# Inverse roots of the norms as exp(-0.5 ln) on ScalarE, with table sets loaded ahead

## What is computed

```python
def rms_norm(x, g):
    xf = x.astype(jnp.float32)
    y = xf * lax.rsqrt(jnp.mean(xf * xf, axis=-1, keepdims=True) + EPS)
    return (y * g.astype(jnp.float32)).astype(x.dtype)

def layer_norm(x, g, b):
    xf = x.astype(jnp.float32)
    mu = xf.mean(-1, keepdims=True)
    var = jnp.square(xf - mu).mean(-1, keepdims=True)
    return ((xf - mu) * lax.rsqrt(var + LN_EPS) * g.astype(jnp.float32) + b.astype(jnp.float32)).astype(x.dtype)
```

## Time and profile before

| | us |
|---|---|
| median of three runs (lowest, highest) | 3767.95 (3752.62, 3784.52) |
| the profiled execution | 3787.55 |
| its span, from the first to the last instruction | 3785.8 |

### The profile page before, as it was taken

The page is one execution under the profiler, slowest core; times in us unless marked ns, Lnnn a source line. Parts: engine busy times, 40 slices in busy tenths (PEclk is TensorE's granted clock), DMA queues, the critical chain, the costliest instruction groups (busy, mean ns, idle before and its releaser), DMA issues. The chain is left out here.

```text
span 3785.8 us, 34815 instructions
## 1 busy us (share of the span) xinstructions
PE 3204.5 (85%) x12250; PEld 2180.1 (58%) x12250; DVE 2147.4 (57%) x3756; ACT 878.0 (23%) x2154; POOL 704.3 (19%) x679
## 2 busy tenths in 40 slices
PE   7999888797777777777777789778999899989998
PEld 6887688583232222232222377366887687668876
DVE  2323577657785764774444562345874454558753
ACT  2112332122222222222222310252220102312201
POOL 0001244003344443443333210000000000100000
PEclk6999888899999999999999999579999997699999
DMA  6657897668999999999999822001332231013321
GB/s 205 205 202 248 280 288 240 211 206 349 421 420 421 419 412 421 418 413 422 421 417 421 342 73 84 0 1 67 95 98 86 70 120 34 1 62 97 97 88 68
DMA packets 154291, 845.76 MB, mean 223 GB/s; under 512 B 15328, under 2 KB 15584, under 8 KB 87584
## 3 DMA queue, kind: packets, MB, share of 16 engines
q0 software_dynamic: 83392, 578.06, 37.5%
q1 hardware_dynamic: 70752, 265.79, 22.0%
HBM read 841.70 MB, written 136.31 MB: 258 GB/s over the span
## 5 line engine op out<-in xcount | busy, mean ns | idle before, releaser
L752 PE MATMUL PS<-AR,HC 128*128 128x512 f32 x1536 | 726.8, 618 | 251.0 <-ACT HC L1190 250.6
L198 PE MATMUL PS<-AR_r,RHI 128*128 128x512 f32 x1888 | 761.4, 403 | 96.0 <-DVE AR_r L1359 60.0
L200 PE MATMUL PS<-AR_r,RING_r 128*128 128x512 f32 x1888 | 745.9, 395 | 0.0
L752 PEld LDWEIGHTS PS<-AR,HC 128*128 128x128 f32 x1536 | 283.3, 194 | 693.6 <-ACT HC L1190 398.6
L1544 DVE SCALAR_TENSOR_TENSOR AR<-AR 128x1024 f32<-128x1024 f32 x384 | 469.9, 1224 | 359.4 <-DMA AR<-peer_uv,XC 358.6
L199 PE MATMUL PS<-AR_r,RHI 128*128 128x512 f32 x1504 | 594.1, 395 | 0.0
L457 POOL DMA_INDIRECT AR<-peer_uv,XC x384 | 402.3, 1048 | 737.4 <-PE PS L752 543.3
L198 PEld LDWEIGHTS PS<-AR_r,RHI 128*128 128x128 f32 x1888 | 362.2, 192 | 183.8 <-issue 87.4
L1341 DVE CAST RHI<-RING 128x1024 fp32r<-128x1024 f32 x256 | 178.7, 698 | 466.9 <-DMA RING<-in_wstream 463.6
L200 PEld LDWEIGHTS PS<-AR_r,RING_r 128*128 128x128 f32 x1888 | 361.7, 192 | 77.2
L199 PEld LDWEIGHTS PS<-AR_r,RHI 128*128 128x128 f32 x1504 | 287.9, 191 | 64.6 <-issue 6.0
(11 more groups left out here) (333 smaller groups left out, 3779.9 us busy)
## 6 DMA issues: line engine op xcount, KB each, us to landing
RING<-in_wstream SPq DMA_DIRECT2D x304, 512.0 KB, 3.6
peer_uv<-in_peer_u SPq DMA_DIRECT2D x48, 1024.0 KB, 12.7
peer_uv<-in_peer_v SPq DMA_DIRECT2D x48, 1024.0 KB, 13.0
peer_uv<-in_peer_v POOLq DMA_DIRECT2D x16, 1024.0 KB, 22.2
peer_uv<-in_peer_u POOLq DMA_DIRECT2D x16, 1024.0 KB, 22.3
AR<-peer_uv,XC POOLq DMA_INDIRECT x384, 13.5
XL<-in_xl SPq DMA_DIRECT2D x1, 2048.0 KB, 9.9
RHI_f<-peer_uv,XC POOLq DMA_INDIRECT x128, 13.5
```

What stands on the lines that cost most here:

```text
L198: pe.matmul(out, sh, mh, start=start, stop=False)
L200: return pe.matmul(out, sl, mh, start=False, stop=stop)
L752: mm = pe.matmul(bank(2 * (tt % 2) + x), DIAG[:, n % NDIAG, :], ROWS_UV[n % NROW][:, D + 512 * x:D + 512 * x + 512], start=(j == 0), stop= ...
```

## The change

`root` becomes an Ln with the same scale and bias, a wait of ScalarE for itself, and an Exp with scale -0.5 in place. What it writes is the inverse root, so all wide reciprocals of VectorE go: in `finish`, in n1 and the context's norm, for both sets of four heads, and for the difference attention's 24 and 8 columns. `preload_act_table_set` puts a table load at a chosen place: the set that has both Ln and Exp is loaded at the start of each `rms` and `layer_norm`, after the Silu of n1, and ahead of both norms of heads; the set that has Silu is loaded ahead of the feed-forward loops. The stick-breaking and the difference attention follow on places where the first of these is held. In the difference attention the root of the first six heads moves from step 30 to step 29 of ScalarE's loop, and the semaphore `root` counts 1 and 2 in place of 1 to 3.

```diff
--- before.py
+++ after.py
@@ -46,6 +46,7 @@
 EPS, LN_EPS = 1e-6, 1e-5
 MASKED = -1e30
 LN_MIN = 2.0 ** -63
+LN_EXP, SILU = "natural_log_exp_and_others", "silu_and_others"
 
 BLK = 8
 NSLOT = 4
@@ -470,7 +471,7 @@
                 barrier(pool, n)
             pool.dma_start(STRIP, t["strips"]).then_inc(s_strip, 16)
             barrier(pool, 15)
-            pool.wait_ge(df["root"], 2)
+            pool.wait_ge(df["root"], 1)
             for h in range(DHALF):
                 for ib in range(TT):
                     o = DO[:, h, P * ib:P * ib + P]
@@ -1009,9 +1010,13 @@
                 act.wait_ge(chunk_used, c + 1)
 
             def root(out, src, scale, eps):
-                return act.activation(out, src, ACT.Sqrt, scale=scale, bias=par(eps))
+
+                steps.done(act.activation(out, src, ACT.Ln, scale=scale, bias=par(eps)))
+                steps.wait()
+                return act.activation(out, out, ACT.Exp, scale=-0.5)
 
             def rms(s, gain, shift, to):
+                act.preload_act_table_set(LN_EXP)
                 for k in range(KT):
                     after(act, s, "res", k + 1, KT)
                     act.activation(ar(S * k, S), XL[:, k, :], ACT.Square).then_inc(s["sq"], 1)
@@ -1268,6 +1277,7 @@
                     act.wait_ge(u["evac"], g * BLK + (2 * FT * l + 4 + x + 1))
                     act.activation(HL[:, x, :], HL[:, x, :], ACT.Silu).then_inc(u["sg"], 1)
 
+                act.preload_act_table_set(SILU)
                 with act.Fori(0, 2 * FT // BLK) as g:
                     for j in range(4):
                         pair(g, j)
@@ -1307,7 +1317,7 @@
                         act.activation(DP[i % 2][x][:, 0:n], bank(2 * (i % 2) + x, 0, n), ACT.Exp,
                                        bias=DNM[:, 2 * i + x:2 * i + x + 1],
                                        accum_out=DRS[:, 2 * i + x:2 * i + x + 1]).then_inc(df["exp"], 1)
-                if i == TT * DHALF + 6:
+                if i == TT * DHALF + 5:
                     head_root(0, DHALF)
                 if 1 <= i <= n_df:
                     k = i - 1
@@ -1369,8 +1379,6 @@
             def finish(s, src, name, x, parts):
 
                 after(dve, s, "root", 1, 1)
-                steps.done(dve.reciprocal(STAT[:], STAT[:]))
-                steps.wait()
                 for k in range(KT + 2):
                     if k < KT:
                         dve.tensor_tensor(HL[:, k, :], src[:, k, :], STAT[:], ALU.mult).then_inc(s["scaled"], 1)
@@ -1392,12 +1400,9 @@
 
             dve.wait_ge(s_in, 80)
             dve.wait_ge(n1["root"], 1)
-            steps.done(dve.reciprocal(STAT[:], STAT[:]))
-            dve.wait_ge(ctx_root, 1)
-            steps.done(dve.reciprocal(SMALL[:], SMALL[:]))
-            steps.wait()
             for k in range(KT):
                 dve.tensor_tensor(HL[:, k, :], XL[:, k, :], STAT[:], ALU.mult).then_inc(n1["scaled"], 1)
+            dve.wait_ge(ctx_root, 1)
             for k in range(KT):
                 dve.tensor_tensor(HC[:, k, :], XC[:, k, :], SMALL[:], ALU.mult).then_inc(ctx_scaled, 1)
             dve.wait_ge(chunk_used, FIRST["mod1"] + 16)
@@ -1507,8 +1512,6 @@
             for h in range(HG_HEADS):
                 o, r = HLF[:, 512 * h:512 * h + 512], EW[:, 512 * h:512 * h + 512]
                 dve.wait_ge(ho["root"], h + 1)
-                steps.done(dve.reciprocal(r, r))
-                steps.wait()
                 steps.done(dve.tensor_tensor(o, o, r, ALU.mult))
                 steps.wait()
                 dve.scalar_tensor_tensor(MIX[:, 4 + h, :], o, par("hg_norm")[:, h:h + 1], G[:, h, :], ALU.mult, ALU.mult)
@@ -1690,8 +1693,6 @@
                                          ).then_inc(rt["dev"], 1)
             for h in range(RET_HEADS):
                 dve.wait_ge(rt["root"], h + 1)
-                steps.done(dve.reciprocal(RST[:, h, :], RST[:, h, :]))
-                steps.wait()
                 steps.done(dve.tensor_tensor(RO[:, h, :], RO[:, h, :], RST[:, h, :], ALU.mult))
                 steps.wait()
                 dve.tensor_tensor(MIX[:, h, :], RO[:, h, :], RG[:, h, :], ALU.mult)
@@ -1843,16 +1844,10 @@
                         ins = dve.scalar_tensor_tensor(DJUNK[ib], o, 1.0, o, ALU.mult, ALU.mult,
                                                        accum_out=DSS[:, TT * h + ib:TT * h + ib + 1])
                     ins.then_inc(df["squares"], 1)
-                if i == TT * DHALF + 7:
-                    dve.wait_ge(df["root"], 1)
-                    dve.reciprocal(DROOT[:, 0:TT * DHALF], DROOT[:, 0:TT * DHALF]).then_inc(df["root"], 1)
                 if n_df - ahead <= i < n_df:
                     split_chunk(FIRST["out_o"] + i - (n_df - ahead))
 
-            dve.wait_ge(df["root"], 3)
-            last = DROOT[:, TT * DHALF:TT * DIFF_HEADS]
-            steps.done(dve.reciprocal(last, last))
-            steps.wait()
+            dve.wait_ge(df["root"], 2)
             for h in range(DHALF, DIFF_HEADS):
                 for ib in range(TT):
                     o = DO[:, h, P * ib:P * ib + P]
```

## The result

The changed kernel takes 3721.2 us (median of 4 runs, 3713.24 to 3739.23), the kernel before 3776.23 (4 runs, 3752.62 to 3791.85). The ratio is 0.9842, with a 95% interval of 0.9807 to 0.9878: 1.6% less, some 60 us; the two medians are 55.0 us apart. The predicted 3723.5 is met within 2.3 us, but partly by luck: the predicted saving was 44.5 from a median of 3767.95, and one run added to the three known ahead lifts that median by 8.3. The profiled execution took 3727.29 us, its span 3725.5 against 3785.8: 60.3 less.

The account below looks back on a forecast made before the run. TensorE was busy for 85% of the span; the change pays in norms where it stands still. Terms 13.5 + 5.4 + 14.2 + 6.9 + 3.8 + 0.4 + 0.3 = 44.5 us, from 3767.95 to 3723.5, range 3698 to 3746.

Parts of the forecast that it names:

- Part 1: n2 and layer norms 0 to 2: root ready before VectorE finishes its splits, so the full reciprocal goes; 13.5 us.
- Part 2: nf and last layer norm: VectorE waits for the root, Exp takes the reciprocal's place; 2.7 each, 5.4 us.
- The price by the rows: Table loads: 1.28 us each, next instruction 0.01 later, without an added drain; so the load ahead of nf fits.
- Part 3: Norms of four heads in series lose load and reciprocals from the chain: retention 14.2 us, the scan's gated norm 6.9.
- The scan's heads: Gated norm ahead of the output projection: same chain as the retention's, but a chunk landing limits the gain to 6.9 us.
- the third of these landed 10.3 us later: Third chunk of the output weights: issued at 675.19, landed at 685.5, a time kept for the changed kernel.
- next in line is nearer: Rival, 0.17: scan's chunks later (5.5 lost), attention starts no sooner (3.8), semaphores at seven norms (1.4); about 34 us gained.
- first term: Scan's norm: chunks land later, as with the fourth chunk, losing 5.5 of the 6.9 us.
- Part 4: Stick-breaking attention: 17 loads, 21.8 us of ScalarE, go; only 3.8 on the path, 2.57 at the head, 1.27 later.
- That is 1.27 more: Stick-breaking attention: in one head of seven a load ends later than the weights; removing it gains 1.27 us.
- the rival with a rising clock: Stick-breaking attention: TensorE's clock rises with shorter pauses, 10 us more, 54 in all, 3713 us; chance 0.18.
- Part 5: Edits worth little: feed-forward loops lose 20 loads for 0.4 us, difference attention gains 0.3, other sites 0.

Follow-up runs that it names:

- stat_only: The kernel before with only the norms of the tokens changed (n2, nf, four layer norms: Ln and Exp, set loaded at each one's start): 3780.51 us.
- two_loads: The changed kernel with two table loads more in each of the six norms of the tokens, behind the wait for the sum: 3718.46 us, profiled.
- copies_only: The changed kernel with three expert table pieces moved from behind the output weights' first chunks to behind the experts' first chunks, keys unmoved: 3748.69 us.
- rt_only: The kernel before with only the retention's norm of heads changed, and the Exp-only set loaded again behind it: 3787.49 us.
- no_preload: The changed kernel with all six preloads left out, so a load comes where a function needs it: 3757.6 us, ratio 0.9925.
- loads_only: The kernel before, norms unchanged, with only the table sets loaded ahead of the stick-breaking attention and the feed-forward loops: 3781.35 us.
- control: The kernel before, unchanged, profiled once more: 3801.39 us, span 3799.6.
- two_loads_again: The changed kernel with two more loads in each of the six token norms, profiled a second time and timed: 3750.52 us, ratio 0.9895.
- keys_later: The changed kernel with GpSimd fetching the expert keys only when the first chunk of the output weights is used: 3741.39 us, ratio 0.9857.
- copies_early: The changed kernel with three expert table pieces moved from behind the output weights' first chunks to behind chunks of the second modulation: 3736.75 us, ratio 0.9839.

## Why the prediction was right, and where it was not

**Part 1, reciprocals behind the chunk splits: right.** Four norms, 3.3 to 3.4 each, and stat_only gives them alone. The slack read above, 0.45 and 2.28 us, which two_loads bears out, is what the part relied on: the Exp is done before VectorE asks.

**Part 2, behind the root: right.** 2.7 twice. The load ahead of nf fitted in: it stands at 2150.06 for 1.28 us, and the squares follow at 2151.61, released by VectorE, not by the load. The price by the rows held; that of the Trainium skill (ScalarE: Activation LUTs, What ACT_TABLE_LOAD costs), by which the load would have stuck out by about 1 us, did not.

**Part 3, the retention's heads: right** (14.3, forecast 14.2), alone and in the whole. **The scan's heads: the right chain, a wrong size.** The step that failed is "the third of these landed 10.3 us later", kept for the changed kernel. Forecast 6.9, measured 3.8: the chunk took 13.4. The prediction held fixed a transfer whose neighbours move: the keys' 1 MB follow the same barrier as VectorE's splits. copies_only shows that transfers hold that wait (7.3 without the three pieces). Of the 3.1 us the keys are some 2.6: at the same spacing of issues, with the same pieces but the keys behind, rt_only's chunk took 10.8. The other 0.5 go with the closer spacing, or are the scatter of such landings (10.3 to 11.0 in the six profiles in which the keys come behind the landing or 1.2 us ahead of it). And no_preload's step of 4.0 has another end than the changed kernel's 3.8: VectorE's chain in the one, the landing in the other. So the rival "next in line is nearer" was right in its first term, with 3.1 of the 5.5 us that it had for it; its other two, 3.8 and 1.4, did not come: TensorE did start the attention's work sooner, and the seven norms show no such loss.

**Part 4, loads in the stick-breaking attention: right at the head, right elsewhere in the number only.** 4.0 in loads_only for 3.8, although ScalarE's busy time falls by 20.5 us there: the loads were covered by TensorE. The head's 2.6 are the two loads. The step "That is 1.27 more" failed: rt_only, stat_only and no_preload keep that load and have 1.39 us of wait there like the rest, so the prediction took for a cost of the load what came from where the low clock fell in two profiles (before and control). In the whole change the attention gives 5.0 to 5.3, at a granted clock of 0.77 in place of 0.75; that is 1.2 us of TensorE's busy time (81.99 to 80.77), and the rival with a rising clock had 10.

**Part 5: right as far as it can be seen.** In the changed kernel the loops are within 0.5 us of before, but for the last down-projection, 1.4 shorter where the unchanged control is 1.5 shorter. The largest difference otherwise is 1.3 us, in two_loads_again.

**The sum.** The steps add to 42.0 for 43.8, one error of 3.1 and the stick-breaking's 1.1 the other way; without the 2.4 of the stick-breaking's rest, of which 1.5 to 2.2 come with the loads kept (rt_only, stat_only), the edits have 39.6. The remaining 18 us of the profiled pair stand at no edit. 7.3 are in the first 650 us, where the control gains 3.6 and the profiles with the changed kernel's code up to there lie between a gain of 0.5 (two_loads) and a loss of 7.6 (keys_later). Another 2.5 came in the unchanged control too (1.1 in the recurrence's matmuls behind 650 us, 1.4 in the last down-projection), so they belong to the one profile of the kernel before. 1.9 go with nf's shorter wait, 2.7 in the retention come and go without it, and the rest are steps of about 1 us or less. The ratios (0.9842, 0.9845, and 0.9839 for the nearly equal copies_early) do lie on more than 42 us: 59 to 61, with intervals whose lower ends are at 37 to 46 us; the differences of the medians are 55.0, 46.6 and 57.5. What fills the gap, if there is one, stays open. TensorE's clock is the only term of that size that the profiles show, in the projections of two_loads and in the difference attention: the stretch took 156.4, 176.7, 159.1, 173.7 and 176.6 us in the five profiles that have its old code and 151.0 to 176.1 in the nine that have the new (five of them 165.6 or 165.7). The means are 168.5 and 163.0, and single values scatter by more than that.

## What to carry to other kernels

Price a wide VectorE reciprocal (3.35 us for 512 columns here) against an Exp on ScalarE (0.63), but read at each site who is late for it: it was worth 3.4, 2.7 or nothing, and 14.3 where four stood in series. The idiom needs a table set with both functions, named by hand: without that half of the gain went. When a shortened wait sits ahead of a landing, list what else the same barrier releases; a transfer measured under the old order is not a constant, and moving its neighbours mostly moved the delay: to the next norm (4.6 and 4.8 us longer than before), or ahead of the stretch. A load, or any wait, that sticks out in one execution may be covered in the next, when TensorE's low clock falls elsewhere: look at a second profile before counting it.

## What was not expected of the hardware

The kernel before, unchanged, spent 156.4 and 176.7 us in the same difference attention, by mean granted clocks of 0.66 and 0.58; one changed kernel spent 195.3 and 220.9 us in the same projections, at 0.98 and 0.86. Both are mixtures of the two levels, 2.4 and 1.2 GHz, and the share of each changes from one execution to the next with no change in the work. The runs of one kernel differ by 20 to 50 us, and their clocks go with it: of the kernel before, the run of 3760.17 us has a mean of 0.933, the one of 3807.52 us 0.918. That is as large as half of the change that was to be judged, or more.
